# An expert layer on one core: the order of the expert pairs is ranked by the rows of each pair's large expert

## The chip, the core and the metric

The kernel runs on one core of a Trainium2 chip. The metric is the time of one execution in microseconds (us), lower is better. Engines are named as the profile names them: PE is TensorE's matrix product, PEld its loading of the stationary operand, DVE is VectorE, ACT is ScalarE, POOL is GpSimd and SP is SyncE, which here does nothing but issue transfers.

## The reference

Two layers work on 384 tokens (128 of a prompt, 256 of a latent grid) of width 1024. Each layer has attention and then a channel mixer. The channel mixer of the second layer is a mixture of eight experts, and each token goes to two of them:

```python
def moe_swiglu(h, w_router, wg, wu, wd):
    logits = (h @ w_router).astype(jnp.float32)
    top_v, top_i = lax.top_k(logits, TOP_K)
    top_p = jax.nn.softmax(top_v, axis=-1)
    gates = jnp.sum(jax.nn.one_hot(top_i, N_EXPERTS, dtype=jnp.float32) * top_p[..., None], axis=-2)
    act = jax.nn.silu(jnp.einsum('bnd,edf->bnef', h, wg)) * jnp.einsum('bnd,edf->bnef', h, wu)
    act = act * gates.astype(h.dtype)[..., None]
    return jnp.einsum('bnef,efd->bnd', act, wd)
```

TOP_K is 2 and N_EXPERTS is 8. Each expert has a gate and an up matrix of 1024 x 2816 and a down matrix of 2816 x 1024, all in 32-bit floats. Which tokens an expert gets is known only when the logits are.

## The kernel before

Attention, the dense channel mixer of the first layer and the router run first. Then `h_table` in device memory holds the rows of the tokens sorted by expert, and a loop goes over the experts (`expert_loop`, with the body `expert` on each engine).

**Sizes and kinds.** VectorE counts each expert's tokens and rounds them up to 32, 64, 96 and so on (`size`, lines 1640 to 1643). An expert's rows are cut into `groups` of 128 rows and a tail of 32 or 64 rows (lines 1669 to 1679); `padded` is the rounded number of rows. An expert with no group of 128 is *little*, one with one or two groups is *large* (two groups with a tail of 64 rows are neither). Expert 0 is outside of this and always comes first (`some` leaves it out).

**Pairs.** A large expert and a little one are worked on together, in one turn of the loop. Both stand in one list of 66 granules, and the supers of the two alternate. A super is 512 of the 2816 hidden columns (the sixth has 256). How many pairs there are is the smaller of the two counts (`counted[:, 2:3]`). What is left over is worked on alone, after the pairs. With `low` (one where the column is smaller than the row) and a sum over the row, line 1691 and line 1695 give `ahead_of`, the number of experts of the same class with a smaller number. That is the place of the expert's pair: the first large expert goes with the first little one, and so on. Lines 1696 to 1741 turn these places into `sched`, a table of whole numbers that every engine reads at the top of a turn: the variant of the body, the first row, the number of the expert.

**The planning's place.** All of this runs on VectorE in one chain of short operations. `link` puts a wait behind an operation, so that the next one starts when its result is there. Behind the planning stand `base_columns(1)` (line 1636), which copies the first expert's columns, and then the first turn. TensorE waits for that copy and for `sched_ready` before its first product of the first turn (line 2612); SP waits for `sched_ready` before it loads the seventeenth granule.

**The ring.** A granule is 1 MiB of weights and is loaded by two transfers of 512 KB. SP loads the granules in the order of use, an expert has 33 of them. The ring holds 16 granules and a half: SP waits until the granule 16 places back is freed (`freed`), then issues. TensorE frees a granule when the last step of its super has read it.

**Steps of a turn.** `steps_of` gives the order of the steps of a turn: for each super the tail of 32 or 64 rows, then each group of 128 rows, once for each half of the super's columns. The first step of a pair is a plain one (line 2634 on TensorE). A group's further steps are taken in two parts each for operand and weight (three products at lines 2368, 2369 and 2372 for gate and up, at 2393, 2396 and 2399 for down). The parts of the weights are made by ScalarE (line 1184) and VectorE (line 1827) from the ring. Tails are taken plainly from the ring: line 2451 for 32 rows, line 2445 for 64. At the third step of a turn ScalarE issues the loads of the rows of the next turn.

**The last turn** is an expert alone (the first and the last turn are singles here, the three between are pairs). Meanwhile GpSimd gathers the finished rows of the other experts and VectorE adds them to the tokens (`fold`, line 1774).

The code waits in this way for a granule and for its place:

```python
            def freed(t, pos):
                kind, _, _, k = granule_of(pos)
                if kind == "gu":
                    sp.wait_ge(gu_freed, t * GU_GRANULES + (k + 1))
...
                for pos in range(AHEAD, GRANULES):
                    freed(t, pos - AHEAD)
                    load_granule(now, pos)
```

Of the kernel before, what the change touches and what calls it, by code (L numbers as in the profile page):

```python
# [22 lines left out]
ALU = mybir.AluOpType  # L23
# [3 lines left out]
P = 128  # L27
# [14 lines left out]
NE = 8  # L42
# [259 lines left out]
def build(nc, x_prompt, x_sample, cache_a_k, cache_a_v, cache_b_k, cache_b_v, c, c_ctx, w_ada,  # L302
# [4 lines left out]
    with ctx:  # L307
# [85 lines left out]
        padded = sb("padded", [P, NE])  # L393
# [5 lines left out]
        wanted = sb("wanted", [P, 2, NE])  # L399
        ahead_of = sb("ahead_of", [P, 2, NE])  # L400
        counted = sb("counted", [P, 4])
        alone = sb("alone", [P, 2, NE])
        leads = sb("leads", [P, NE])
# [36 lines left out]
        compared = small[:, 4 * NE * NE:6 * NE * NE].rearrange("p (n a e) -> p n a e", n=2, a=NE)  # L440
# [842 lines left out]
        def _(dve):  # L1283
# [3 lines left out]
            def link(ins):  # L1287

                chain[0] += 1
                ins.then_inc(dve_step, 1)  # L1290
                dve.wait_ge(dve_step, chain[0])
# [325 lines left out]
            low = cst[:, C_LOW:C_LOW + 64]  # L1617
# [15 lines left out]
            def base_columns(n):  # L1633
# [16 lines left out]
                                          scalar=1.0, in1=base[:, :].unsqueeze(1).broadcast_to([P, NT, NE]),  # L1650
                                          op0=ALU.add, op1=ALU.add))
# [15 lines left out]
            order_of = cst[:, C_ORDER + NE:C_ORDER + 2 * NE]  # L1667
            odd_turn = cst[:, C_ORDER + 2 * NE:C_ORDER + 3 * NE]
            link(dve.tensor_scalar(groups[:, :], size[:, :], 2.5, None, ALU.is_gt))
            for g in range(2, 4):  # L1670
# [16 lines left out]
            dve.scalar_tensor_tensor(out=little, in0=size[:, :], scalar=1.5, in1=some, op0=ALU.is_lt, op1=ALU.mult)  # L1687
            link(dve.scalar_tensor_tensor(out=large, in0=size[:, :], scalar=1.5, in1=some, op0=ALU.is_gt, op1=ALU.mult))
            link(dve.scalar_tensor_tensor(out=large, in0=size[:, :], scalar=7.5, in1=large, op0=ALU.is_lt, op1=ALU.mult))
            dve.tensor_reduce(counted[:, 0:2], wanted[:, :, :], AX, ALU.add)  # L1690
            link(dve.tensor_tensor(compared, wanted[:, :, :].unsqueeze(2).broadcast_to([P, 2, NE, NE]),
                                   low.rearrange("p (e f) -> p e f", e=NE).unsqueeze(1).broadcast_to([P, 2, NE, NE]),
                                   ALU.mult))
            dve.tensor_tensor(counted[:, 2:3], counted[:, 0:1], counted[:, 1:2], ALU.min)
            link(dve.tensor_reduce(ahead_of[:, :, :], compared, AX, ALU.add))
            link(dve.scalar_tensor_tensor(out=wanted[:, :, :], in0=ahead_of[:, :, :], scalar=counted[:, 2:3],
                                          in1=wanted[:, :, :], op0=ALU.is_lt, op1=ALU.mult))
            rest, rest_turn = alone[:, 0, :], alone[:, 1, :]
# [978 lines left out]
```

## Time and profile before

| | |
|---|---|
| median of 3 runs | 1712.25 us |
| lowest and highest run | 1708.8 and 1712.45 us |
| the profiled execution, its own time | 1710.32 us |
| its span in the profile | 1708.5 us |
| PE busy | 1548.9 us (91%) |
| DVE busy | 759.8 us (44%) |
| ACT busy | 555.6 us (33%) |
| moved by the transfers | 432.20 MB |
| the five turns of the expert loop | 852.6 to 1678.4 us of the span |

The profiled execution has 1.8 us outside of its span. Busy shares are means over the whole span; the transfers are slow in the first half (attention and dense layer) and fast in the second. "PEclk" is the share of the full clock that TensorE was granted. In a row of a timeline the bracket holds the idle time of the engine before the row and what ended it.

### The profile page before, as it was taken

How to read it: one execution, taken by the hardware profiler on the slowest of the kernel's cores; microseconds unless marked ns; L12 is line 12 of the kernel's file. 1: busy time of each engine (PE TensorE's matmuls, PEld its weight loads, DVE VectorE, ACT ScalarE, POOL GpSimd, SP SyncE). 2: the span in 40 equal slices, each digit the busy share in tenths (PEclk: the TensorE clock that was granted, in tenths of full speed). 3: DMA queues.
4: the chain of work that ended last, by engine and by line, in shares of the span. 5: the costliest groups of instructions: out<-in, count | busy, mean ns of one | idle time of the engine just before them, and what ended most of it. 6: DMA issues, size and time to landing. Idle time of an engine off the chain costs nothing. (4 is left out here: it accounts for less than half of the span.)

```text
span 1708.5 us, 24835 instructions
## 1 busy us (share of the span) xinstructions
PE 1548.9 (91%) x9206; PEld 1028.5 (60%) x9207; DVE 759.8 (44%) x1231; ACT 555.6 (33%) x965; POOL 88.8 (5%) x109
## 2 busy tenths in 40 slices
PE   4798989999999799899688898989999899999895
PEld 1684567788888487457423565655556577677422
DVE  0483776333332655675601353444345433243224
ACT  0432554333332343460201343423344333233101
POOL 2010002200000011000100000000000000000002
PEclk8899999999999899999889999999999999999997
DMA  9244535934432623640999999999999488787992
GB/s 347 100 146 166 198 124 177 343 128 146 148 110 87 222 99 131 229 149 25 389 390 380 371 388 395 386 390 376 377 393 386 169 296 295 275 294 261 366 363 101
DMA packets 206624, 432.20 MB, mean 253 GB/s; under 512 B 11880, under 2 KB 52840, under 8 KB 206224
## 3 DMA queue, kind: packets, MB, share of 16 engines
q1 hardware_dynamic: 195712, 390.64, 63.2%
q0 software_dynamic: 7712, 29.05, 4.7%
q10 hardware_dynamic: 3056, 10.62, 1.8%
q8 instruction: 87, 1.43, 0.3%
q14 instruction: 57, 0.47, 0.1%
HBM read 409.55 MB, written 20.71 MB: 252 GB/s over the span
## 5 line engine op out<-in xcount | busy, mean ns | idle before, releaser
L2043 PE MATMUL ps<-d_ring_parts,scratch_parts 128*128 128x512 f32 (+1 forms) x444 | 171.6, 386 | 14.6 <-DVE hT_parts L1326 9.8
L2445 PE MATMUL ps<-ring,hT 128*64 128x512 f32 (+1 forms) x512 | 112.8, 584 | 22.4 <-issue 11.3
L2451 PE MATMUL ps<-ring,hT 128*32 128x256 f32 x1760 | 118.0, 385 | 12.9 <-DMA ring<-in_w_moe_up 10.8
L2043 PE MATMUL ps<-gu_ring_parts,scratch_parts 128*128 128x512 f32 (+1 forms) x336 | 128.1, 381 | 0.0
L1864 DVE TENSOR_TENSOR cst<-cst,ps 128x256 f32<-128x256 f32 (+2 forms) x89 | 32.8, 369 | 194.8 <-ACT cst L1159 194.8
L2043 PE MATMUL ps<-d_ring_parts,hT_parts 128*128 128x512 f32 (+1 forms) x312 | 118.6, 380 | 0.0
L1184 ACT ACTIVATE qkv_parts<-ring 128x1024 fp32r<-128x1024 f32 x102 | 103.1, 1049 | 13.0 <-issue 13.0
L2043 PEld LDWEIGHTS ps<-d_ring_parts,scratch_parts 128*128 128x128 f32 x444 | 84.5, 190 | 33.2 <-issue 9.3
L2043 PE MATMUL ps<-gu_ring_parts,o_parts 128*128 128x512 f32 x264 | 103.8, 393 | 0.0
L1167 ACT ACTIVATE cst<-ps 128x128 f32<-128x128 f32 (+1 forms) x51 | 16.1, 315 | 235.4 <-PE ps L2467 224.5
L2451 PEld LDWEIGHTS ps<-ring,hT 128*32 128x32 f32 x1760 | 55.4, 110 | 60.5 <-issue 14.6
L2445 PEld LDWEIGHTS ps<-ring,hT 128*64 128x64 f32 x512 | 36.0, 143 | 86.1 <-issue 67.8
L1827 DVE TENSOR_TENSOR odd_parts<-ring,qkv_parts 128x1024 fp32r<-128x1024 f32 x52 | 61.9, 1221 | 56.6 <-PE ps L2451 34.0
L1159 ACT ACTIVATE cst<-ps 128x256 f32<-128x256 f32 (+2 forms) x89 | 30.6, 344 | 165.4 <-PE ps L2372 74.7
L1827 DVE TENSOR_TENSOR even_parts<-ring,qkv_parts 128x1024 fp32r<-128x1024 f32 x50 | 59.5, 1222 | 51.3 <-ACT qkv_parts L1184 18.8
L1975 PE MATMUL ps<-gu_ring,small 128*32 128x512 f32 x384 | 57.9, 697 | 22.3 <-DMA x<-in_x_sample 17.4
L2368 PE MATMUL ps<-qkv_parts,o_parts 128*128 128x512 f32 x174 | 72.8, 418 | 5.4 <-DVE even_parts L1827 5.4
L2043 PEld LDWEIGHTS ps<-gu_ring_parts,scratch_parts 128*128 128x128 f32 x336 | 64.1, 191 | 12.6
L1589 DVE TENSOR_TENSOR scratch_parts<-ps,scratch_parts 128x256 fp32r<-128x256 f32 x33 | 14.0, 425 | 126.2 <-ACT scratch_parts L1031 126.2
L2369 PE MATMUL ps<-qkv_parts,hT_parts 128*128 128x512 f32 x174 | 68.6, 394 | 0.0
L911 ACT ACTIVATE d_ring_parts<-gu_ring 128x2048 fp32r<-128x2048 f32 (+1 forms) x26 | 46.0, 1778 | 64.6 <-PE ps L2043 64.6
L1320 DVE TENSOR_TENSOR gu_ring_parts<-gu_ring,d_ring_parts 128x2048 fp32r<-128x2048 f32 (+1 forms) x26 | 55.2, 2127 | 26.2 <-ACT d_ring_parts L911 25.6
(398 smaller groups left out, 3135.5 us busy)
## 6 DMA issues: line engine op xcount, KB each, us to landing
ring<-in_w_moe_gate SPq DMA_DIRECT2D x176, 512.0 KB, 9.8
ring<-in_w_moe_up SPq DMA_DIRECT2D x176, 512.0 KB, 11.5
ring<-in_w_moe_down SPq DMA_DIRECT2D x176, 512.0 KB, 10.2
gu_ring<-in_w_ada SPq DMA_DIRECT2D x48, 1024.0 KB, 7.4
gu_ring<-in_w_in SPq DMA_DIRECT2D x16, 1024.0 KB, 7.3
gu_ring<-in_w_ffn_gate SPq DMA_DIRECT2D x11, 1024.0 KB, 5.5
gu_ring<-in_w_ffn_up SPq DMA_DIRECT2D x11, 1024.0 KB, 8.1
d_ring<-in_w_ffn_down SPq DMA_DIRECT2D x11, 1024.0 KB, 10.0
```

What stands on the lines that cost most here:

```text
L911: act.activation(hi, value, ACT.Copy).then_inc(weight_hi, 1)
L1159: act.activation(hid_e[0:rows, k % 2, 0:f], ps[0:rows, 6 + k % 2, 0:f], ACT.Silu).then_inc(sil_ready, counted_to(k))
L1184: act.activation(hi_slots[i % HI_SLOTS].rearrange("p (q f) -> p q f", q=4), raw, ACT.Copy).then_inc(sub_hi, 1 if i < len(subs) - 1 else 1 ...
L1320: dve.tensor_tensor(lo, value, hi.bitcast(F32), ALU.subtract).then_inc(weight_lo, 1)
L1827: dve.tensor_tensor(low, raw, hi_slots[i % HI_SLOTS].rearrange("p (q f) -> p q f", q=4).bitcast(F32), ALU.subtract).then_inc(sub_lo, 1 if ...
L1864: dve.tensor_tensor(hid_e[0:rows, k % 2, 0:f], hid_e[0:rows, k % 2, 0:f], ps[0:rows, 6 + k % 2, f:2 * f], ALU.mult).then_inc(hid_ready, 1 ...
L1975: pe.matmul(ps[g:g + CT, piece_bank(l, j), :], cond[:, kc, :], w[:, kc, :], start=(kc < 4), stop=(kc >= 4 and kc < KD - 1))
L2043: ins = pe.matmul(out, a, w, start=(start and n == 0), stop=(stop and n == 2))
L2368: pe.matmul(bank, t_hi, w_hi, start=(kc == 0), stop=False)
L2369: ins = pe.matmul(bank, t_lo, w_hi, start=False, stop=False)
L2445: ins = pe.matmul(ps[64 * j:64 * j + 64, bank, 0:2 * f].rearrange("p (a f) -> p a f", a=2), hT[:, kc, col:col + 64], wt[:, :, f * j:f * j ...
L2451: ins = pe.matmul(ps[32 * j:32 * j + 32, bank, 0:FC].rearrange("p (a f) -> p a f", a=2), hT[:, kc, col:col + 32], wt[:, :, P * j:P * j + P ...
```

## The change

The rank of a large expert among its class no longer comes from its number. A weight of 8 times the padded rows less the expert's number is formed, for large experts only. The expert with the largest weight keeps rank 0. An expert with k larger ones ahead of it, k above 0, gets the rank n - k, where n is the number of large experts: the smallest of the others comes second, then upwards. The ranks of the little experts are formed as before. Nothing else differs; the other engines have the same instructions.

```diff
             link(dve.scalar_tensor_tensor(out=large, in0=size[:, :], scalar=7.5, in1=large, op0=ALU.is_lt, op1=ALU.mult))
+            weight = leads[:, :]
+            link(dve.scalar_tensor_tensor(out=weight, in0=padded[:, :], scalar=8.0, in1=order_of,
+                                          op0=ALU.mult, op1=ALU.subtract))
             dve.tensor_reduce(counted[:, 0:2], wanted[:, :, :], AX, ALU.add)
-            link(dve.tensor_tensor(compared, wanted[:, :, :].unsqueeze(2).broadcast_to([P, 2, NE, NE]),
-                                   low.rearrange("p (e f) -> p e f", e=NE).unsqueeze(1).broadcast_to([P, 2, NE, NE]),
-                                   ALU.mult))
+            link(dve.tensor_tensor(weight, weight, large, ALU.mult))
+            dve.tensor_tensor(compared[:, 0], weight.unsqueeze(1).broadcast_to([P, NE, NE]),
+                              weight.unsqueeze(2).broadcast_to([P, NE, NE]), ALU.is_gt)
+            link(dve.tensor_tensor(compared[:, 1], little.unsqueeze(1).broadcast_to([P, NE, NE]),
+                                   low.rearrange("p (e f) -> p e f", e=NE), ALU.mult))
             dve.tensor_tensor(counted[:, 2:3], counted[:, 0:1], counted[:, 1:2], ALU.min)
             link(dve.tensor_reduce(ahead_of[:, :, :], compared, AX, ALU.add))
+            behind = alone[:, 0, :]
+            link(dve.tensor_scalar(behind, ahead_of[:, 0, :], -1.0, counted[:, 0:1], ALU.mult, ALU.add))
+            link(dve.scalar_tensor_tensor(out=ahead_of[:, 0, :], in0=ahead_of[:, 0, :], scalar=0.5, in1=behind,
+                                          op0=ALU.is_gt, op1=ALU.mult))
             link(dve.scalar_tensor_tensor(out=wanted[:, :, :], in0=ahead_of[:, :, :], scalar=counted[:, 2:3],
                                           in1=wanted[:, :, :], op0=ALU.is_lt, op1=ALU.mult))
```

The instructions of VectorE at this place, in the planning between `large` and the first use of `ahead_of`, before:

```order
L1689 SCALAR_TENSOR_TENSOR wanted<-size,wanted 128x8
L1690 TENSOR_REDUCE counted<-wanted 128x2
L1691 TENSOR_TENSOR small<-wanted,cst 128x128
L1694 TENSOR_TENSOR counted<-counted 128x1
L1695 TENSOR_REDUCE ahead_of<-small 128x16
L1696 SCALAR_TENSOR_TENSOR wanted<-ahead_of,counted,wanted 128x16
```

The same place in the changed kernel, where `leads` holds the weight, `small` the comparisons and `alone` the value of `behind`:

```order
L1689 SCALAR_TENSOR_TENSOR wanted<-size,wanted 128x8
L1691 SCALAR_TENSOR_TENSOR leads<-padded,cst 128x8
L1693 TENSOR_REDUCE counted<-wanted 128x2
L1694 TENSOR_TENSOR leads<-leads,wanted 128x8
L1695 TENSOR_TENSOR small<-leads 128x64
L1697 TENSOR_TENSOR small<-wanted,cst 128x64
L1699 TENSOR_TENSOR counted<-counted 128x1
L1700 TENSOR_REDUCE ahead_of<-small 128x16
L1702 TENSOR_SCALAR alone<-ahead_of,counted 128x8
L1703 SCALAR_TENSOR_TENSOR ahead_of<-ahead_of,alone 128x8
L1705 SCALAR_TENSOR_TENSOR wanted<-ahead_of,counted,wanted 128x16
```

Five instructions are added: two for the weight, one because the comparison of 128 elements is now two of 64, and two for the turned rank. The order in which the turns run is not in this listing: every engine holds one body for each variant and branches by the table at run time.

## Rows read from the trace of the kernel before

**Rows 1.** The page: busy times, and the 40 slices of the span.
```profile
PE 1548.9 (91%) x9206; PEld 1028.5 (60%) x9207; DVE 759.8 (44%) x1231; ACT 555.6 (33%) x965; POOL 88.8 (5%) x109
...
GB/s 347 100 146 166 198 124 177 343 128 146 148 110 87 222 99 131 229 149 25 389 390 380 371 388 395 386 390 376 377 393 386 169 296 295 275 294 261 366 363 101
```

**Rows 2.** Busy time by turn of the expert loop: window, length, engines, clock, DMA share, GB/s.
```profile
852.60:931.76 79.16, 67.67 (x300) 22.76 (x300) 3.78 (x8) 7.07 (x16) 0.00 (x0) 0.91 1.04 384
931.76:1124.10 192.34, 174.33 (x1498) 111.06 (x1499) 86.36 (x102) 75.20 (x112) 0.00 (x0) 0.98 1.05 387
1124.10:1327.22 203.12, 197.62 (x1256) 112.04 (x1256) 89.90 (x108) 76.62 (x112) 0.00 (x0) 1.00 1.04 384
1327.22:1602.99 275.77, 265.93 (x1916) 187.64 (x1917) 107.33 (x136) 89.60 (x141) 0.00 (x0) 0.99 0.75 271
1602.99:1678.40 75.41, 64.09 (x291) 21.57 (x291) 15.72 (x19) 4.39 (x12) 7.43 (x9) 0.95 0.91 331
```

**Rows 3.** The same windows for line 2368 alone: PE busy (count), PEld busy (count).
```profile
931.76:1124.10 192.34, 33.60 (x80) 15.02 (x80) 0.98 1.05 387
1124.10:1327.22 203.12, 33.68 (x80) 15.01 (x80) 1.00 1.04 384
1327.22:1602.99 275.77, 70.29 (x168) 32.07 (x168) 0.99 0.75 271
```

**Rows 4.** The page, DMA issues: KB each, microseconds to landing.
```profile
ring<-in_w_moe_gate SPq DMA_DIRECT2D x176, 512.0 KB, 9.8
```

**Rows 5.** Waits of TensorE, 931.8 to 1124.1 us: total, times, longest.
```profile
PE ps L2451 <- DMA ring<-in_w_moe_up: 10.8, 7, 2.1
```

**Rows 6.** Timeline of TensorE, 1003 to 1079 us: start, duration, idle before.
```profile
1005.09 1.07 PE L2451 MATMUL ps<-ring,hT 128*32 128x256 f32 x16 [1.64 <-DMA ring<-in_w_moe_up]
...
1038.35 1.07 PE L2451 MATMUL ps<-ring,hT 128*32 128x256 f32 x16 [2.07 <-DMA ring<-in_w_moe_up]
...
1075.62 1.07 PE L2451 MATMUL ps<-ring,hT 128*32 128x256 f32 x16 [0.80 <-DMA ring<-in_w_moe_up]
...
1078.33 0.85 PE L2451 MATMUL ps<-ring,hT 128*32 128x256 f32 x12 [1.65 <-DMA ring<-in_w_moe_up]
```

**Rows 7.** Timeline of SyncE's queue, 1324 to 1372 us.
```profile
1327.77 1.13 SPq L724 DMA_DIRECT2D ring<-in_w_moe_up  x1
1370.14 1.71 SPq L730 DMA_DIRECT2D ring<-in_w_moe_down  x3
```

**Rows 8.** Timeline of TensorE: where the second and fourth turn start to free their first super.
```profile
951.81 0.80 PE L2368 MATMUL ps<-o_parts 128*128 128x512 f32 x1
...
1368.42 0.39 PE L2368 MATMUL ps<-qkv_parts,o_parts 128*128 128x512 f32 x1
```

**Rows 9.** SyncE's loads into the ring issued from 1365 to 1372 us.
```profile
DMA to landing us min/median/max: 3.7/4.4/5.6
```

**Rows 10.** Waits of TensorE, 1603.0 to 1678.4 us.
```profile
PE ps L2445 <- DMA ring<-in_w_moe_up: 6.1, 3, 3.4
```

**Rows 11.** Waits of TensorE, 820 to 936 us.
```profile
PE ps L2612 <- issue: 8.4, 1, 8.4
PE ps L2445 <- DMA ring<-in_w_moe_up: 5.0, 3, 2.8
```

**Rows 12.** Timeline of VectorE, 840 to 851 us: the planning.
```profile
840.58 0.17 DVE L1689 SCALAR_TENSOR_TENSOR wanted<-size,wanted 128x8 f32<-128x8 f32 x1
...
840.87 0.28 DVE L1691 TENSOR_TENSOR small<-wanted,cst 128x128 f32<-128x128 f32 x1
...
850.14 0.68 DVE L1636 COPY hT<-ps 128x512 f32<-128x512 f32 x1
```

**Rows 13.** Busy time by window, second part of the second turn.
```profile
1000.00:1124.10 124.10, 110.86 (x989) 71.72 (x988) 58.10 (x68) 51.35 (x77) 0.00 (x0) 1.00 1.05 390
```

**Rows 14.** The chain that ended last: the long piece in the last turn.
```profile
1615.47 9.85 DMA small<-y_rows,row_at
```

**Rows 15.** Timeline of TensorE: its last wait for the ring.
```profile
1668.63 1.93 PE L2445 MATMUL ps<-ring,hT 128*64 128x256 f32 x12 [1.89 <-DMA ring<-in_w_moe_up]
```

## The prediction

> **What bounds the kernel now.** I read the page first, to find where the time could move. TensorE is busy for 91% of the span, and the transfers run at 370 to 395 GB/s in twelve slices from the twentieth on, then fall to 169 and to 261 to 296 in the five after that [rows 1]. So the expert loop has two regimes, and the change only reorders it. I therefore cut the loop at the first product of each turn and asked for the windows [rows 2]. The reader is to see four things there. The first turn takes 79.16 us. The three pairs take 192.34, 203.12 and 275.77 us. The first two move 387 and 384 GB/s, the third only 271. The last turn takes 75.41 us.
>
> I call the pairs A, B and C in the order of now. Line 2368 tells their sizes: 80 split products in A, 80 in B, 168 in C [rows 3]. So C has two groups of 128 rows and A and B one. B is longer than A by its tail. By the diff the largest comes first, then the smallest: the new order is C, A, B. Each pair keeps its little partner only by place; all three have a 32-row one, so a pair's work does not depend on which it gets.
>
> What is each pair bound by? A granule is two transfers of 512 KB [rows 4], so 1.05 MB, which at 387 GB/s takes 2.71 us. A pair is 66 granules, 178.8 us. C takes 97 us more than its weights need, B 24 more, A 13.5 more. The waits of TensorE say that only A is late by the transfers: 10.8 us in 7 waits for the ring [rows 5]. They stand in three places [rows 6]: one of 1.64 us at 1003 us, four between 1036 and 1047 (10.8 less the rest, 6.7), and two of 0.80 and 1.65 at 1075 and 1077.
>
> Why there? A follows the first turn, which eats the ring empty: that turn itself waits 5.0 us for the ring at its end [rows 11]. C follows B and finds the ring full: SP issues the last granule that has a place at 1327.77, half a microsecond after C's first product, and the next one at 1370.14 [rows 7]. For 42 us it is shut out, by a pair that would not have needed a lead.
>
> **The change, part by part.**
>
> *C moves from fourth to second turn.* It starts with a nearly empty ring. Its first super is read by more steps than A's, and A in that place needed no granule that was late until 1003 us, 72 us in [rows 6]. C asks for 66 granules in 275.77 us, 4.18 us each, against 2.71 supplied. I cost its waits at 0; what hides the transfers is C's own products, and its idle SP time shrinks. If the cover were thin, the bound is what A pays there at most, but C asks at two thirds of A's pace.
>
> *A moves from second to third turn* and finds the ring full. A full ring is not worth its 16 granules for the whole turn, since SP is shut out until A's first super is freed. That begins with the first split product, 20.05 us after A's first product (951.81 less 931.76) [rows 8, 2]. In C, where that step comes later, SP's issue follows its first product by 1.72 us (1370.14 less 1368.42) [rows 7, 8], and the granule lands 4.4 us later [rows 9]. So granule 16 lands 26.2 us into the turn. From there 2.71 us for each, and 4.1 us once for the 384 rows of the next turn (1.57 MB by their shape). Against that stand A's wants, each with the waits before it taken off:
> - first place, granule 27: there at 60.1 us, wanted at 71.7. The 1.64 us go.
> - second place, granules 39 to 42: there from 92.6 to 100.8, wanted from 102.9. The 6.7 us go.
> - third place, granules 53 and 54: there at 130.6 and 133.3, wanted at 134.7 and 135.8. The margin of 2 to 4 us is inside what I leave out (a place that is freed late holds up the whole row of loads). Ends are 0 and 2.45 us gained; I take half, 1.2.
>
> That is 9.5. A wait also splits a run of products, which costs beyond itself. Upper bound for everything: A is idle for 192.34 less 174.33, 18.0 us, and B for 5.5 [rows 2]; if A came down to B, 12.5. Between 9.5 and 12.5 I take **11.0**; low end 8.3 (third place stays, no extra).
>
> *B moves from third to fourth turn.* It had no waits for the ring, and starts after A, as now. 0. It is long enough (203.12 against 178.8) to let the transfers run 24 us ahead, 9 granules.
>
> *The last turn now follows B, not C.* C hands it a full ring; it waits 6.1 us all the same [rows 10], for places that are freed late. Now C finds the same after B: all 16 issued half a microsecond into the turn [rows 7]. So B hands over the same. 0. Beside it runs the chain of gathers, 9.85 us for one [rows 14]; it starts when the last pair's rows are stored, three blocks in B as in C.
>
> *Five more operations on VectorE.* They stand in the linked chain before the copy at 850.14 [rows 12], and TensorE's first product at 852.59 waits for that chain (8.4 us idle) [rows 11]. The nearest rows are 0.17 us for 8 elements and 0.28 for 128 [rows 12], so between 0.85 and 1.4 us; the split comparison gives some back; I take 1.0. SP and ScalarE also wait for the table, but the first sixteen granules are still landing. The first turn's 5.0 us of waits for the ring [rows 11] take the 1.0 up, as the transfers run at 384 GB/s through that turn [rows 2] whether TensorE is early or not. So 0. If that cover is gone, +1.0.
>
> *The clock.* A's turn was granted 0.98 and C's 0.99 [rows 2]; the second part of A, with all seven waits, 1.00 [rows 13]. So the waits cost no clock, and removing them gives none back. What A lost in its beginning (0.02 of 192 us, 3.8) may belong to the place after the first turn, and then C pays it. Net 0, ends -3.8 and +3.8.
>
> **Sum.** -11.0 against the profiled execution's 1710.32 gives 1699.3. The median of the runs is 1.9 above that execution, so for a median I say 1701.2, rounded **1701**. Gain at most 12.5 + 3.8 = 16.3 (1696.0); at least 8.3 - 1.0 - 3.8 = 3.5 (1708.7).
>
> **The rivals.** About 0.2% (3.4 us) is what a measurement of this kernel can tell from no change.
>
> *The ring is too short to carry the lead.* A's own time is about 180 us (192.34 less 12), its weights need 178.8, and while SP is shut out for some 25 us nine granules are lost. If places freed late push the supply back by the 10 us of margin at the second place, only the first wait goes: 1712.25 less 1.6, 1710.6. For it: the last turn waits 6.1 us with a full ring [rows 10]. Against it: that turn asks for 33 granules in 75 us, 2.3 us each, A for one each 2.7. The Trainium skill (Perfetto Trace Analysis, Optimization Strategy) says that the same gap repeating on the engine that should be saturated can mean too little room for the next tile; by that the gaps would stay under any order, and the time would be this rival's.
>
> *More than I say.* If TensorE-bound and transfer-bound turns simply even out, the last turn's 6.1 us of waits [rows 10] go too: 1701.2 less 6.1, 1695.1. Against it: nothing in that turn's beginning changes. The same page and section of the Trainium skill says that where the most-contended engine changes over time, interleaving the regimes may improve the performance; the trace has these regimes [rows 2].
>
> *Slower: the last turn starves.* TensorE gets the last granule it waits for at 1668.63 [rows 15], 65.6 us into the turn, and ends it 9.8 us later. With n granules landed at its start the last lands (33 - n) x 2.71 us in. If B handed over as few as 3, that is 81.3, 15.7 later, and 1701.2 becomes 1717. The point from which it decides: the gain of 11 is gone when (33 - n) x 2.71 is over 77, so n under 5. Against it: B's 24 us of surplus alone bring 9 granules.
>
> *The order does not change.* Then 1712.3 plus at most 1.0, 1713. Against it: C's count is twice the others' [rows 3], and the weight is 8 times the rows, so a tie can't hide it.
>
> **How the numbers follow.** Forecast 0.80 (its own range 1696 to 1708.7), ring too short 0.09, more 0.05, starving 0.04, order unchanged 0.02. Faster takes the forecast and the second rival, 0.85. Slower takes the starving and half of the unchanged order (its 1.0 us may become more), 0.05. The rest, 0.10, is the same. A range of 1695 to 1708.7 leaves out the first, third and fourth rivals, 0.15; this is under 0.2, and I round it to 1695 to 1709.
>
> **What would show it.** In the new profile the turns' counts on line 2368 read 168, 80, 80. C takes about 276 us from 932 on, at over 290 GB/s, and SP is not shut out in its first 60 us. A takes 180 to 182 us with at most 2.5 us of waits for the ring. B takes 203 and the last turn 75. The copy of line 1636 comes at about 851.1, and the second turn begins where it began. I am wrong if A still waits over 5 us for the ring, if C waits for it in its first supers or takes over 280 us, or if the last turn takes over 80.

## The result, and the profile of the changed kernel

The changed kernel takes **1703.11 us** (median of 5 runs, 1698.71 to 1704.46) against 1712.45 for the kernel before (5 runs, 1708.8 to 1713.45). The ratio is 0.9932, with a 95% interval of 0.9912 to 0.9953. The gain is 9.3 us by the medians and 11.6 by the ratio. The profiled execution took 1703.7 us, its span is 1701.9, 6.6 below the span before. A second set of 6 runs of the same kernel (experiment 9) gives 1702.72 and 0.9938 [0.9921, 0.9955].

Lines behind the diff stand 9 lines further down in the changed kernel: line 2445 of before is 2454, 2451 is 2460, 2368 is 2377, 2612 is 2621, 2634 is 2643, 1741 is 1750. In the kernels with a table of constants (experiments 1 to 4 and 11) they stand another 2 lines further down.

The page answers to [rows 1]. The slices of weak transfer (238 to 331 GB/s) now stand ahead of those at 376 to 394, where before they stood behind them:

```profile
PE 1555.7 (91%) x9206; PEld 1034.7 (61%) x9207; DVE 760.2 (45%) x1236; ACT 555.3 (33%) x965; POOL 88.5 (5%) x109
...
GB/s 347 102 138 174 195 127 165 347 146 140 149 116 82 223 99 128 214 170 25 358 364 377 346 280 297 331 291 263 238 376 392 393 391 380 379 394 381 391 352 95
```

The windows by turn answer to [rows 2], with the same columns (window and its length, then the busy time of PE, PEld, DVE, ACT and POOL, each with its count, then the granted clock, the DMA share and GB/s). The last window ends 1.3 us behind the last product of its turn:

```profile
856.11:933.78 77.67, 66.31 (x299) 22.32 (x300) 3.78 (x8) 7.06 (x16) 0.00 (x0) 0.92 1.00 367
933.78:1205.83 272.05, 265.04 (x1916) 187.17 (x1917) 104.14 (x130) 88.97 (x140) 0.00 (x0) 0.99 0.84 306
1205.83:1386.45 180.62, 171.90 (x1498) 110.88 (x1499) 89.53 (x109) 75.42 (x114) 0.00 (x0) 0.99 0.96 353
1386.45:1592.90 206.45, 197.71 (x1256) 112.05 (x1256) 90.68 (x108) 76.59 (x112) 0.00 (x0) 1.00 1.04 386
1592.90:1670.00 77.10, 67.31 (x291) 22.30 (x291) 14.49 (x16) 4.97 (x13) 7.41 (x9) 0.90 0.90 335
```

Line 2377, which was 2368 in [rows 3], gives the order of the pairs by its counts:

```profile
933.78:1205.83 272.05, 70.03 (x168) 31.93 (x168) 0.99 0.84 306
1205.83:1386.45 180.62, 33.61 (x80) 15.01 (x80) 0.99 0.96 353
1386.45:1592.90 206.45, 33.67 (x80) 15.01 (x80) 1.00 1.04 386
```

The order is C, A, B. Now the budget, by the starts of the turns:

| stretch | before | after | difference |
|---|---|---|---|
| first product of the loop | 852.59 | 856.11 | +3.5 |
| first turn | 79.17 | 77.67 | -1.5 |
| A | 192.34 | 180.62 | -11.7 |
| B | 203.12 | 206.45 | +3.3 |
| C | 275.77 | 272.05 | -3.7 |
| last turn and what follows | 105.51 | 109.00 | +3.5 |
| span | 1708.5 | 1701.9 | -6.6 |

The three pairs gave 12.1 us. The two ends took 5.5 of it back. The experiments had to say which of these rows belong to the order.

**The waits for the ring.** In A's turn (1205.8 to 1386.5 us) the row that read 10.8 us in 7 waits [rows 5] reads:

```profile
PE ps L2460 <- DMA ring<-in_w_moe_up: 1.5, 1, 1.5
```

The timeline shows where it is, 134.6 us into the turn:

```profile
1340.47 1.07 PE L2460 MATMUL ps<-ring,hT 128*32 128x256 f32 x16 [1.47 <-DMA ring<-in_w_moe_up]
```

That is the third place of [rows 6]. The first two places are gone. SyncE's queue shows why, and answers to [rows 7]: A now starts with all places given out, and SP issues nothing for 19.4 us.

```profile
1205.54 1.34 SPq L724 DMA_DIRECT2D ring<-in_w_moe_up  x1
1226.26 1.71 SPq L730 DMA_DIRECT2D ring<-in_w_moe_down  x3
```

In the last turn (1592.9 to 1670 us) the row of [rows 10] has halved, from 6.1 us to 3.3, and yet the turn is no shorter (75.8 us from its first product to the end of its last, where it was 75.4):

```profile
PE ps L2454 <- DMA ring<-in_w_moe_up: 3.3, 2, 2.8
```

What took the 2.8 us is TensorE's busy time, 64.09 us before [rows 2] and 67.31 now for the same products. The difference stands at the start of the turn. Its first 10 us, before and after, at a granted clock of 1.00 and 0.73 (the two levels are 2.4 and 1.2 GHz):

```profile
1602.99:1612.99 10.00, 7.09 (x32) 2.28 (x32) 0.81 (x2) 0.00 (x0) 0.00 (x0) 1.00 0.96 337
```

```profile
1592.90:1602.90 10.00, 9.71 (x32) 2.87 (x32) 0.00 (x0) 0.24 (x1) 0.00 (x0) 0.73 1.04 404
```

The same 32 products take 2.6 us longer. TensorE asks for the later granules that much later, and waits less for them.

**B's 3.3 us are not work.** TensorE's busy time in B is 197.71 us against 197.62 [rows 2]. What differs is the idle time in the bracket of the next turn's first product, since the windows run from start to start. Before, the row behind B is the first here and the row behind C the second:

```profile
1327.22 3.27 PE L2634 MATMUL ps<-ring,hT 128*128 128x512 f32 x7 [1.74 <-issue]
...
1602.99 3.23 PE L2612 MATMUL ps<-ring,hT 128*64 128x512 f32 x14 [3.15 <-issue]
```

After, the first is behind C and the second behind B:

```profile
1205.83 2.41 PE L2643 MATMUL ps<-ring,hT 128*128 128x512 f32 x5 [0.93 <-issue]
...
1592.90 7.57 PE L2621 MATMUL ps<-ring,hT 128*64 128x512 f32 x22 [4.91 <-issue]
```

The step from the last pair to the single last turn costs more than a step between pairs. Behind C it went from 3.15 to 0.93 (2.2 of C's 3.7), behind B from 1.74 to 4.91 (3.2, all of B's change). Which pair stands last moves this idle time and hardly changes its sum: +1.0. But behind the longer idle time of 4.91 us TensorE's clock was lower, as shown above, and this adds the 2.6 us. The other 1.5 us of C lie in the first 36 us of its turn.

### The profile page after: what moved, and what is told of

Read it like the earlier page. It is cut to its first block, busy times and chain, and to the rows that moved or that the text cites. A ratio compares the mean times of both kernels' runs of the same rounds, so it can differ in the third digit from the quotient of the medians.

```text
span 1701.9 us, 24840 instructions
## 1 busy us (share of the span) xinstructions
PE 1555.7 (91%) x9206; PEld 1034.7 (61%) x9207; DVE 760.2 (45%) x1236; ACT 555.3 (33%) x965; POOL 88.5 (5%) x109
## 4 chain that ended last, share of the span: by engine, by line
issue 47%; PE 40%; DVE 6%; DMA 5%; ACT 2%; SPq 0%; POOL 0%; DVEq 0%; ACTq 0%; POOLq 0%
PE ps L2052 27%; PE ps L1984 3%; DMA small<-y_rows,row_at 2%; PE ps L2146 2%; DMA gu_ring<-in_w_ada 1%; PE ps L2111 1%; DMA d_ring<-in_w_ffn_down 1%; PE ps L2124 1%; PE ps L1987 1%; DVE gu_ring_parts L1320 1%; PE ps L1996 1%; PE ps L2008 1%; DVE smax L1412 1%; PE ps L2224 0%; PE ps L2598 0%
## 6 DMA issues: line engine op xcount, KB each, us to landing
ring<-in_w_moe_gate SPq DMA_DIRECT2D x176, 512.0 KB, 10.4
ring<-in_w_moe_up SPq DMA_DIRECT2D x176, 512.0 KB, 11.3
```

## The experiments

The theory, called the supply theory below: **A's gain is the supply of granules it inherits**. A pair that follows the first turn finds a ring that is behind, a pair that follows another pair finds a full one. The rivals of the prediction (a ring too short to carry a lead, a last turn that starves) stay to be tested, and a third came with the trace: the last turn ends by something other than the transfers.

### 1 to 4. Other orders by a table of constants

The five operations of the change stay, but the weight comes from the table of constants, so that any order can be had:

```diff
-            link(dve.scalar_tensor_tensor(out=weight, in0=padded[:, :], scalar=8.0, in1=order_of,
-                                          op0=ALU.mult, op1=ALU.subtract))
+            link(dve.scalar_tensor_tensor(out=weight, in0=padded[:, :], scalar=0.0,
+                                          in1=cst[:, C_RANK:C_RANK + NE], op0=ALU.mult, op1=ALU.add))
```

and, for the order A, B, C (the other orders differ in the three values):

```diff
+    c[:, [C_RANK + 1, C_RANK + 4, C_RANK + 6]] = [3.0, 1.0, 2.0]
```

**1. order_abc**, the old order with the new operations.

> The changed kernel, but the weight comes from a table of constants made for these data, so that the pairs run in the old order A, B, C. It has all five added operations and none of the reordering. Supply theory: the time of the kernel before, between 0 and +1.0 us (the operations cost 0.85 us of VectorE's chain, the first turn's waits for the ring take most of it up); pair A again waits about 10.8 us for the ring in 7 waits. Rival (the gain came from something else in the new code, such as another layout): the gain of the changed kernel, -9 us, stays.

Measured: 1712.72 us (12 runs), ratio 1.0011 [0.9993, 1.0029], so +1.9 us with an interval of -1.2 to +5.0. A takes 192.79 us with 8.3 us of waits for the ring (10.8 were expected). The operations alone give nothing; the gain is the order.

**2. order_acb.**

> The same with the order A, C, B. Supply theory: A still follows the first turn and finds an empty ring, so it keeps its 10.8 us of waits; B ahead of the last turn is enough for that turn. No gain: 0 to +1 us against before. Rival (what is lost is the 42 us in which SyncE is shut out while C runs its first super, and any place for C further forward wins part of it): a gain of 3 to 6 us.

Measured: 1715.25 us (12 runs), ratio 1.0012 [0.9998, 1.0027], so +2.1 us, where 0 to 1 was expected. C no longer stands fourth, behind B, and nothing is gained: A behind the first turn waits for the ring again.

```profile
PE ps L2462 <- DMA ring<-in_w_moe_up: 8.7, 7, 1.6
```

**3. order_bac.**

> The same with the order B, A, C. Supply theory: B is enough to run the transfers ahead (203 us against 179), so A loses its waits down to 0 to 2.5 us and the gain is that of the changed kernel, -9 to -12 us, though C runs last of the pairs and finds a full ring as before. Rival (C must be early, where its slow start needs no lead): no gain or at most 3 us.

Measured: 1704.79 us (12 runs), ratio 0.9959 [0.9941, 0.9976], 7.0 us faster, with an interval of 4.1 to 10.1; 9 to 12 were expected. C is fourth, as it was before. It is enough to take A from behind the first turn: A takes 184.77 us, and its waits read

```profile
PE ps L2462 <- DMA ring<-in_w_moe_up: 1.1, 2, 0.9
```

**4. order_cba.**

> The same with the order C, B, A, from the largest down. A has no waits of note, but uses its lead up, and the last turn, which asks for a granule every 2.3 us, follows it. Supply theory: the last turn's waits for the ring grow from 6 us to 15 to 20, and the sum is +1 to +4 us against before. Rival (the last turn is set by its chain of gathers, not by the ring, so a late ring costs it nothing): the gain of the changed kernel, -9 us.

Measured: 1709.27 us (12 runs), ratio 0.9977 [0.9959, 0.9995], 4 us faster. The sign was wrong. Its mechanism was there, in the last turn (1589.0 to 1675.9 us):

```profile
PE ps L2456 <- DMA ring<-in_w_moe_up: 12.8, 7, 3.9
```

A hands over little, and the last turn waits 12.8 us where it waited 6.1 [rows 10]. It is 86.87 us to the start of the next stage, 8.3 more than the 78.57 before, against A's gain of 8.0 (184.3) and C's of 3.8 (272.0). The working behind the expectation had only A's gain and the last turn's loss. It left out that C is shorter in second place, that B is 1.1 shorter, and that what follows the last turn is 25.4 us and not 26.9 (experiment 8 tells why).

What follows from the four: A costs 192.3 to 193.6 us behind the first turn (three kernels), 180.6 behind C in third place, 184.8 behind B in third and 184.3 behind B in fourth place. The 4 us between 180.6 and the other two are not waits for the ring, which read 1.5, 1.1 and 1.3 us. In fourth place 3.6 us are the dearer step to the last turn (5.1 us of idle time ahead of it, where B's first product behind A has 1.5). In third place behind B, 2.3 are idle time and 1.9 busy time. The supply theory stands for the waits, which are 9.3 of A's 11.7 us. The rival that C in fourth place is what costs falls with 2 and 3.

### 5 and 6. A shorter ring

```diff
-AHEAD = 16
+AHEAD = 14
```

**5. ahead14_before**, in the kernel before.

> The kernel before with a lead of 14 granules where it had 16 (the wait for a granule's place asks for the granule 14 places back to be freed). Theory (each turn is paid by how many granules its predecessor hands over, and how early its own supers free their places): every turn that waits for the ring now waits longer, the second turn (A, behind the first) most. Worked out by laying each turn's wants against a supply of 2.71 us for each granule: +9.5 us, 1722, of which the second turn 3 to 5 and the last turn 2 to 4; TensorE's waits for the ring rise from 22 us over the five turns to over 30. Rival (the ring is longer than it needs to be, and the waits are the landing time of single transfers, not places): no change, within 2 us.

Measured: 1723.55 us (12 runs) against 1713.07, ratio 1.0055 [1.0037, 1.0074]: 9.4 us slower by the ratio, where 9.5 was expected. The waits in the first, second and last turn are 8.3, 9.6 and 9.3 us, 27 together where 22 stood and over 30 were expected. A waits no longer than before (193.44 us), against the expectation; the loss is in the first turn (83.73 against 79.17) and the last.

**6. ahead14_after**, in the changed kernel.

> The changed order with a lead of 14 granules where it had 16. Theory (what the order gives is a full ring handed to A, so it is worth less with a shorter ring): the same working gives 1716.5 to 1718 us, +4 to +5 against the kernel before at 16 and +13 against the changed kernel at 16, so that the gain of the order shrinks from 9 to about 5 us; A waits for the ring again, 4 to 7 us. Rival 1 (the order is worth its 9 us whatever the lead, since it only moves A away from the first turn): 4 to 9 us of gain stay in full, 1713 or less when the kernel before is at 1722. Rival 2 (the lead makes no difference): 1703.

Measured: 1713.11 us (12 runs), ratio 1.0002 [0.9981, 1.0023] to the kernel before at 16. Against experiment 5 it is 10.4 us faster by the medians, 9.1 by the ratios; the intervals of the two are 3.1 and 3.6 us to each side, so the totals cannot tell 5 from 9, and rival 1 is not excluded by them. The turn of A can. Its waits in the two kernels of the shorter ring, experiment 5 first:

```profile
PE ps L2451 <- DMA ring<-in_w_moe_up: 9.6, 8, 2.2
```

```profile
PE ps L2460 <- DMA ring<-in_w_moe_up: 5.6, 5, 2.0
```

A goes from 193.44 to 187.67 us, 5.8 gained where 11.7 were gained with 16 granules. So the lead that A carries is worth what the ring holds of it, as the theory says. C gained 4.2 and the tail 2.1 in this pair of profiles, and B lost 3.2, which is why the total did not shrink with A. The expectation counted A alone.

### 7. early_copy: is the copy on the path?

```diff
             dve.tensor_copy(sched[:, :], table_f[:, :, :].rearrange("p a n -> p (a n)")).then_inc(sched_ready, 1)
+            dve.tensor_copy(numbers, iota)
+            base_columns(1)
...
-            dve.tensor_copy(numbers, iota)
-            base_columns(1)
```

> The changed kernel with the copy of the first expert's columns (line 1636, and the copy of the numbers that stood ahead of it) moved to right behind the end of the planning, ahead of work that TensorE's first product doesn't need. The first product comes 1.5 to 2.5 us earlier. Theory (the first turn is paced by the transfers, so it covers what comes earlier or later ahead of it): the first turn's waits for the ring grow from 4.9 to about 6 to 7 us and the second turn begins less than 1 us earlier; the time is 0 to 1.0 us lower, 1702 to 1703. Rival (the first turn covers only part, as its time shrank by 1.5 of 3.5 us when it began later): the second turn begins 1.2 to 1.5 us earlier and the time is 1.0 to 1.5 lower. Rival 2 (no cover at all): 2.0 to 2.5 lower, which would mean that the five added operations cost their full 0.8 us.

Measured: 1699.58 us (6 runs), ratio 0.9913 [0.9883, 0.9942], not to be told from the changed kernel. The premise was false, as VectorE's timeline of the two shows, the changed kernel first:

```profile
851.31 0.20 DVE L1750 CAST sched<-table_f 128x70 int32<-128x70 f32 x1
...
853.67 0.68 DVE L1636 COPY hT<-ps 128x512 f32<-128x512 f32 x1
```

```profile
853.07 0.20 DVE L1750 CAST sched<-table_f 128x70 int32<-128x70 f32 x1
...
853.32 0.68 DVE L1636 COPY hT<-ps 128x512 f32<-128x512 f32 x1
```

The first product comes at 856.11 and at 857.83. That is 4.80 and 4.76 us behind the cast to `sched`, though the copy stands 2.1 us nearer to the cast in the second. TensorE's first product follows the **table**, with the copy well inside that time. This kernel does the same work at the same pace as the changed one, and I use its profile as another sample of it. Whether the first turn covers a later start, which this edit was to show, it could not show.

### 8. fold_two: what ends the last turn?

```diff
-HI_SLOTS = 7
+HI_SLOTS = 6
...
-        early_rows = small[:, 0:D]
+        early_rows = [small[:, 0:D], qkv_flat[:, 7168:7168 + D]]
...
-                if m:
-                    pool.wait_ge(folded, 2 * m)
-                pool.indirect_dma_start(early_rows, None, y_rows[0:ROWS_MAX, :],
+                if m > 1:
+                    pool.wait_ge(folded, 2 * m - 2)
+                pool.indirect_dma_start(early_rows[m % 2], None, y_rows[0:ROWS_MAX, :],
```

and the two operations of `fold` take the same buffer. The second buffer lies where the fourth of four slots for parts of operands lay, which goes from the list.

> The changed kernel with two buffers for the rows gathered in the last turn where it had one, so that a gather no longer waits for the addition of the one before (one of the seven buffers for the parts of operands is given up for it). Theory (the last turn ends when its chain of gathers and additions ends, not when its transfers do, which is why the waits for the ring at its start are paid back by less waiting later): the gathers run side by side with the additions, the end of the chain comes 3 to 10 us earlier, and the time falls by 3 to 5 us against the changed kernel, 1698 to 1700; the wait of TensorE at the very end (5.3 us for VectorE) goes. The lost buffer costs 0 to 2 us in the pairs. Rival (the last turn ends with its products, and the transfers pace these): no gain in the last turn, and 0 to 2 us slower by the lost buffer, 1703 to 1705.

Measured: **1696.66 us** (6 runs, 1696.2 to 1699.51), ratio 0.9897 [0.9874, 0.9920]. That is 6.4 us under the changed kernel's own median, more than expected, 2.9 under experiment 7 on the same chip, and the smallest spread of all kernels here. The lost buffer costs nothing that can be seen (the three pairs take 658.77 us together against 659.12).

How the gathers bound the last turn is in the chain of the changed kernel:

```profile
1607.66 9.09 DMA small<-y_rows,row_at
...
1619.67 7.41 DMA small<-y_rows,row_at
...
1630.00 7.68 DMA small<-y_rows,row_at
...
1640.60 8.30 DMA small<-y_rows,row_at
```

Each waits for the addition of the one before; a fifth and a sixth follow in the same way, with 4.1 us of other waiting ahead of the fourth addition. The same pieces in the profile of early_copy, whose last turn begins 1.4 us later, took 8.52, 6.04, 8.15 and 6.98 us. These four are 32.5 us in one profile and 29.7 in the other, and TensorE waits for their end. With two buffers the chain ends with TensorE's own products, and the last turn now waits for the ring instead: 6.9 us in two waits, the longest

```profile
1657.15 3.47 PE L2454 MATMUL ps<-ring,hT 128*64 128x256 f32 x16 [6.66 <-DMA ring<-in_w_moe_up]
```

Before the change, too, TensorE stood idle behind the turn's last product until the chain was done, for 3.18 us. A granule that comes late costs nothing as long as TensorE still ends ahead of that chain. So the 2.8 us less of waiting could not have made the kernel faster, even without the lower clock that used them up.

**What the two buffers give in the profile** is less than the medians say. From the start of the last turn to the end of the kernel fold_two takes 104.2 us, where the three profiles with one buffer take 109.0 (the changed kernel), 103.8 (early_copy) and 103.5 (experiment 9). So the two buffers save the late chain of the first, and nothing against the other two: TensorE's products in the last turn end 3.1 us later than with one buffer (78.9 us into it, and not 75.8), by the waits for the ring. The rest of what sets this profile apart lies ahead of the edit: its first product comes at 853.84, where the three have 856.11, 857.83 and 860.42. Experiment 9 returns to this. By its ratio this kernel is not to be told from experiment 7.

**What a late chain costs behind itself** is in the next products, of lines 2598 and 2607. The changed kernel in its profiled execution:

```profile
1674.05 0.90 PE L2591 MATMUL ps<-cst 128*128 128x128 f32 x3 [5.30 <-DVE cst L1798]
1674.93 6.27 PE L2598 MATMUL ps<-x,cst 128*128 128x512 f32 x8
```

The windows over these products, the changed kernel and then its second profile (experiment 9), give the granted clock, 0.57 and 1.00:

```profile
1674.05:1681.20 7.15, 7.15 (x12) 2.92 (x12) 3.05 (x3) 0.49 (x1) 0.00 (x0) 0.57 0.01 5
```

```profile
1676.82:1681.31 4.49, 4.15 (x12) 1.75 (x12) 3.05 (x3) 0.49 (x1) 0.00 (x0) 1.00 0.02 5
```

### 9. after_again: the changed kernel once more, beside 10 and 11

> The changed kernel once more, as the measure beside the next two on the same chip. Its runs so far lie at 1698.7 to 1699.0 and at 1703.1 to 1704.5. Theory (the last turn ends with the chain of gathers and additions, and where that chain is late TensorE's clock is down for the products behind it, so that being 2.5 us late costs another 2.5): the runs spread over some 5 us again, median 1700 to 1704, and a profile shows the tail at 27.9 us with the products of the final stage at half the clock, or at 25.3 without. Rival (the spread is in the part ahead of the expert loop, whose end moved by 4 us between profiles): the tail is the same in all, and the first product's time tells fast from slow.

Measured: 1702.72 us (6 runs, 1699.6 to 1705.81), ratio 0.9938 [0.9921, 0.9955]. Both the tail and the start of the loop differ between profiles, so each of the two readings holds half. The tail of this profile:

```profile
1676.82 0.55 PE L2591 MATMUL ps<-cst 128*128 128x128 f32 x3 [2.52 <-DVE cst L1798]
1677.70 3.67 PE L2598 MATMUL ps<-x,cst 128*128 128x512 f32 x8 [0.34 <-DVE qkv L1909]
```

TensorE waited 2.52 us here and not 5.30, kept its clock, and the last turn with what follows took 103.5 us and not 109.0. But this profile is no faster: its first product came at 860.42, 4.3 us later, and nothing ahead of that point belongs to the change or to the tail. The start of the first planning operation (line 1640) lies between 833.0 and 841.2 us in the eight profiles in which I read it. The three without the change are at 833.0, 834.1 and 834.7, the five with its operations as they are at 834.0, 834.6, 836.8, 838.5 and 841.2. The five kernels with the table of constants (1 to 4 and 11), which have the same operations, bring their first product at 850.3 to 853.5 us, as the kernels without them do (851.4 to 852.9). What makes the planning start late is on the trace: TensorE's clock in the products of the router. In the 14 us ahead of line 1640 the granted clock was 0.64, 0.50 and 0.64 in the three late profiles (836.8, 841.2, 838.5), and 0.97 to 0.99 in the five others. The kernel before, and then the changed kernel:

```profile
820.11:834.11 14.00, 11.62 (x103) 11.14 (x102) 6.78 (x25) 5.72 (x13) 0.27 (x1) 0.97 1.03 400
```

```profile
822.82:836.82 14.00, 13.75 (x85) 13.35 (x85) 5.86 (x24) 3.73 (x8) 0.00 (x0) 0.64 1.03 396
```

The router's last 18 products begin at 826.59 and at 826.37, so all of the 2.7 us arise behind that point, in work that the two kernels share. They are not a cost of the change. Why the clock fell there in three profiles and not in the others stays open.

### 10 and 11. Two buffers under other orders

**10. fold_before**: the edit of experiment 8 in the kernel before.

> The kernel before (old order, A, B, C) with the two buffers for gathered rows, and nothing of the change. Theory (its last turn too ends with the chain of gathers): 3 to 6 us under the kernel before, 1707 to 1709, the tail from 26.9 to about 25.4 us, and the waits for the ring in the last turn up from 6.1 to about 9. The two edits then add up: the changed kernel with two buffers is 1696.7, another 10 to 12 lower. Rival (the two buffers gain only where the last turn follows B and begins with its ring fuller): 0 to 1 us, 1712.

Measured: 1708.64 us (12 runs) against 1713.69, ratio 0.9976 [0.9963, 0.9990], 4.1 us faster (1.7 to 6.3). The tail is 25.42 us against 26.94. The waits for the ring in the last turn are 7.3 us, not 9. From the start of the last turn to the end its profile takes 102.8 us, 2.7 less than the kernel before. So the kernel before ended by the gathers too. The two gains are 4.1 and 11.6 us by the ratios, and the kernel with both is 17.6 faster; within their intervals they add up.

**11. fold_cba**: the same edit with the order C, B, A.

> The two buffers with the order C, B, A by a table of constants. Theory (behind A the last turn is paced by the transfers, 12.8 us of waits for the ring, and the chain of gathers ends within it): nothing of the two buffers' gain is left, 1707 to 1710 as the same order had with one buffer, last turn 86 to 87 us and tail 25.4. It is then 11 to 13 us slower than the two buffers under the changed order. Rival 1 (the gathers and the ring's transfers slow each other, and two buffers ease that): 1702 to 1705. Rival 2 (the last turn's end is always the gathers): 1701 to 1704, last turn under 83 us.

Measured: 1708.88 us (12 runs), ratio 0.9984 [0.9968, 1.0001], against 1709.27 and 0.9977 of the same order with one buffer. Nothing of the gain is left, as the theory said. In the last turn (1588.1 to 1679.4 us):

```profile
PE ps L2456 <- DMA ring<-in_w_moe_up: 12.5, 5, 3.9
```

The turn takes 91.34 us, more than the 86 to 87 expected, at a granted clock of 0.84. Behind A the last turn is bound by transfers, and here the starving rival can be seen: 12.2 us between this kernel and fold_two by the medians, 12.5 between the last turns of the two profiles. Not all of it is starving. TensorE waits 5.6 us more for the ring and is busy 6.9 us longer with the same products, at the lower clock.

## Why the prediction was right, point by point

**Total.** 1701.0 was forecast, with a range of 1695 to 1709, and 1703.11 came. The order, the turn that gains and the size of its gain were right. Four terms that stood at 0 were not 0. In the profiles they are C (-3.7), B (+3.3), the start of the second turn (+2.0) and the last turn with what follows (+3.5), +5.1 in sum, so that 6.6 us are left of A's 11.7. That the medians came within 2.1 us of the forecast all the same is partly luck, since it depends on how often the executions meet a late start and a late chain.

- *A, -11.0.* Measured -11.7 in the profile. The waits fell by 9.3, for 9.5 worked out, and the working by granules held at each step. SP issues its first load 20.4 us into the turn (1226.26 less 1205.83), where 20.05 was taken from the kernel before. The first two places went. The third place was the doubtful one, "wanted at 134.7", and one wait of 1.5 us is left 134.6 us into the turn. I took half of its 2.45 us and got 1.0. The other 2.4 us are busy time (174.33 to 171.90). The forecast had 1.5 for them and named the splitting of runs of products. By the products, 1.5 of them arise in A's first 30 us, where the granted clock was 0.94 before and 1.00 after, ahead of any wait for the ring, and 0.9 at the places of the old waits. The sum was right here partly by luck.
- *The ring is too short to carry the lead (0.09).* Wrong at 16 granules, and right in kind: at 14, half of A's gain is gone (5.8 for 11.7). The rule of the Trainium skill that stood beside it (Perfetto Trace Analysis, Optimization Strategy: repeating gaps can mean too little room for the next tile) has its evidence in experiment 5, 9.4 us for two granules. But the gaps went with the order as well, at the same room. The other rule of the Trainium skill in that section, that interleaving regimes may improve the performance, agrees with the result: A's 7 waits of 10.8 us became one of 1.5.
- *C moved, 0.* Its 272.05 us without one wait for the ring and 306 GB/s are as forecast. The 3.7 us gained were not forecast: 2.2 are the dearer step to the last turn, which C no longer pays. The claim that SP is not shut out in C's first 60 us fell. It issues nothing for 16.4 us from 958.9 on, and no wait for the ring follows.
- *B moved, 0.* Measured +3.3, the same step paid by B. The text looked at what B hands over in granules and not at what the handover itself costs. With C's 2.2 the mistake in idle time is 1.0 us; what it did to the clock comes under the last turn.
- *Last turn, 0.* "C hands it a full ring, B hands over the same" was right. What failed is the assumption below it, that its waits of 6.1 us are what sets its length. They fell to 3.3, and two things kept the time. The turn now starts behind 4.91 us of idle time at a granted clock of 0.73, and TensorE is busy 3.2 us longer. And the chain of gathers ends last. It was named beside the turn and never priced; experiment 10 puts 4.1 us on it (1.7 to 6.3). Its start follows TensorE's first step: the first gather was issued 12.48 us into the last turn before and 14.76 after. The second rival ("more": the 6.1 us go too) could not pay for this reason.
- *Five operations, +1.0.* From the start of line 1669 to the copy of line 1636, 11.81 us became 12.65, so +0.84; the five read 0.15 to 0.23 us each.

```profile
843.39 0.17 DVE L1691 SCALAR_TENSOR_TENSOR leads<-padded,cst 128x8 f32<-128x8 f32 x1
...
844.66 0.23 DVE L1702 TENSOR_SCALAR alone<-ahead_of,counted 128x8 f32<-128x8 f32 x1
```

- *"The first turn takes the 1.0 up, whether TensorE is early or not".* Half right. The first turn took up 1.5 of 3.5 us in the changed kernel's profile and 2.0 of 7.8 in experiment 9. Its waits hardly fell, from 5.0 to 4.9 and 4.5. Its 20th to 30th microsecond in the kernel before, the changed kernel and experiment 9 show less supply the later it began:

```profile
872.60:882.60 10.00, 10.00 (x50) 3.36 (x48) 0.42 (x1) 0.77 (x2) 0.00 (x0) 1.00 1.04 380
```

```profile
876.10:886.10 10.00, 10.00 (x48) 3.37 (x49) 0.42 (x1) 0.77 (x2) 0.00 (x0) 1.00 0.71 244
```

```profile
880.40:890.40 10.00, 10.00 (x50) 3.29 (x48) 0.42 (x1) 0.77 (x2) 0.00 (x0) 1.00 0.54 178
```

  I read it so, and no experiment tested it: the later TensorE begins, the sooner SP has filled the ring and must wait for TensorE to free a place, and the supply then moves with TensorE. The cover was some 2 us deep at most, enough for the 0.84, which experiment 1 agrees with, and not for more.
- *The clock, 0.* The pairs as a whole were granted 0.99, 0.99 and 1.00, but A's start gained 1.5 us by it. It does not hold for the start of the last turn (2.6 us lost), nor behind the last turn, which the text did not look at.
- *Starving last turn (0.04).* Not in this order. Experiment 11 shows that it exists, behind A.

Of the difference between the 12.1 us of the pairs and the 6.6 of the two profiled spans, 2.0 are the later start net of the first turn (3.5 less 1.5). Of the 3.5, 2.7 come from the router's clock (experiment 9) and 0.84 from the five operations. The other 3.5 are in the last turn and behind it: 2.3 are the later first gather, 0.3 the rest of the chain, 0.9 the clock of the products behind it. The gathers were not slower than before the change: the first four take 32.5 us here and 33.1 in the kernel before. They were slower than in experiment 9, where they take 29.2.

## What to carry to other kernels

Where a ring feeds one engine, cost a new order turn by turn. Ask when the turn's last predecessor hands over how many filled places, and when the turn itself frees its first one; that gave A's gain to within 1 us. Then ask of the last turn which of its chains ends last, since a wait that another chain hides is neither loss nor gain. Here that second question, asked late, gave 4.1 us on the kernel before (1.7 to 6.3). Two buffers for the gathered rows with the changed order have the lowest median of the study, 1696.66 us, though part of that may be an early start of the loop. Price also what a step between bodies costs, by the idle time ahead of the first product and by the granted clock behind it.

## What the chip showed that was not expected

**TensorE's clock behind a short wait.** Ahead of the final stage TensorE waits for VectorE. Where that wait was 2.52 and 2.75 us (experiments 9 and 7), the next eight products took 3.67 us. Where it was 3.18, 3.58 and 3.59 us (the kernel before, experiments 3 and 5), the clock was lower and they took 5.37 us in the first and 5.88 in the last. Where it was 5.30 and 5.38 (the changed kernel, experiment 1), they took 6.27 and 6.15 us. In experiment 2 it was 5.70 and 5.49 us, so the length of the wait alone does not set the price. So 2.8 us of lateness in the gathers went with about 2.6 more in TensorE. The start of the last turn shows the same. Where the idle time ahead of it was 2.88 to 3.19 us (the kernel before, experiments 5 and 10), its first 32 products took 7.09 us; with 2.93 and 3.01 us (experiments 1 and 3) they took 8.78. With 4.81 to 5.21 us, in seven profiles, they took 9.68 to 9.86, and with 4.86 us in experiment 2 they took 8.77. Here too the length of the wait alone does not set the price. The Trainium skill says (Perfetto Trace Analysis, Matmul Optimizations) that the engine scales its power with its utilization, so matmuls should run back to back; the trace agrees, by these rows.

**A transfer of 512 KB into the ring can take well over its median.** In fold_two the load behind the 6.66 us wait took 18.0 us from issue to landing by the chain, where the three kinds of loads into the ring have medians of 10.1 to 11.3. With one buffer the load at that place is slow too: issued at 1640.86, its product begins 15.6 us later. Gathers run beside it in both. That they are the cause was not tried.
